# Up projection of a gated feed-forward by seven block products, with z kept in DRAM

## The reference

```python
def conv_ffn(h, w_up, conv_w, conv_b, w_down):
    s = h.shape[1]
    u = h @ w_up                                   # 1024 -> 2 x 2816
    up = jnp.pad(u, ((0, 0), (CONV_WIDTH - 1, 0), (0, 0)))
    c = conv_b
    for j in range(CONV_WIDTH):
        c = c + conv_w[j] * up[:, j:j + s]
    a, g = jnp.split(c, 2, axis=-1)
    return (jax.nn.silu(a) * g) @ w_down           # 2816 -> 1024
...
x = x + conv_ffn(rmsnorm(x, ffn_norm[l]), w_up[l], conv_w[l], conv_b[l], w_down[l])
```

## Time and profile before

| | us |
|---|---|
| median of 3 runs | 1857.29 (1854.81 to 1857.45) |
| profiled execution, its own time | 1854.01 |
| span of its instructions | 1852.2 |
| PE busy | 1758.5 (95%) |
| VectorE, ScalarE, GpSimd busy | 718.8, 576.9, 618.6 |
| mean granted TensorE clock | 0.981 of full |

### The profile page before, as it was taken

The page is one execution under the profiler, slowest core; times in us unless marked ns, Lnnn a source line. Parts: engine busy times, 40 slices in busy tenths (PEclk is TensorE's granted clock), DMA queues, the critical chain, the costliest instruction groups (busy, mean ns, idle before and its releaser), DMA issues. The chain is left out here.

```text
span 1852.2 us, 23370 instructions
## 1 busy us (share of the span) xinstructions
PE 1758.5 (95%) x8889; PEld 1437.3 (78%) x8889; DVE 718.8 (39%) x1328; ACT 576.9 (31%) x1059; POOL 618.6 (33%) x527
## 2 busy tenths in 40 slices
PE   4799999999889799999999998999999999999999
PEld 3677887877668688888888886888888888888887
DVE  5734334358874302200255222423424433442343
ACT  4435555444454323222112313221221222122121
POOL 4243564644322122222245523322331431333122
PEclk9899999999999999999999998999999999999999
DMA  5301002012200143332454502201210210220002
GB/s 192 107 18 46 25 10 63 1 35 50 67 13 1 25 115 97 106 93 80 132 165 155 184 1 80 80 14 55 68 45 23 68 54 14 68 68 27 18 24 91
DMA packets 118271, 119.29 MB, mean 64 GB/s; under 512 B 15340, under 2 KB 95916, under 8 KB 118188
## 3 DMA queue, kind: packets, MB, share of 16 engines
q1 hardware_dynamic: 118188, 118.16, 20.9%
HBM read 101.25 MB, written 16.89 MB: 64 GB/s over the span
## 5 line engine op out<-in xcount | busy, mean ns | idle before, releaser
L1900 PE MATMUL ps<-act_hi,f_hi 128*128 128x512 f32 x704 | 278.0, 395 | 6.3 <-DVE f_lo L1665 6.3
L1900 PE MATMUL ps<-act_hi,f_lo 128*128 128x512 f32 x704 | 276.9, 393 | 0.0
L1900 PE MATMUL ps<-act_lo,f_hi 128*128 128x512 f32 x704 | 274.6, 390 | 0.0
L1665 POOL TENSOR_TENSOR f_lo<-ffn_area,f_hi 128x1024 fp32r<-128x1024 f32 x65 | 155.3, 2419 | 87.5 <-ACT f_hi L1746 87.5
L1855 DVE TENSOR_TENSOR attn_out<-ps,attn_out 128x512 f32<-128x512 f32 x160 | 106.5, 686 | 136.4 <-PE ps L1920 136.4
L1900 PEld LDWEIGHTS ps<-act_hi,f_hi 128*128 128x128 f32 x704 | 132.9, 189 | 33.7 <-DVE f_lo L1665 6.7
L1900 PEld LDWEIGHTS ps<-act_hi,f_lo 128*128 128x128 f32 x704 | 132.8, 189 | 30.6
L1900 PEld LDWEIGHTS ps<-act_lo,f_hi 128*128 128x128 f32 x704 | 132.7, 189 | 29.8
L1565 PE MATMUL ps<-act_hi,g_hi 128*128 128x512 f32 x384 | 152.0, 396 | 3.1 <-DVE g_lo L1500 3.1
L1565 PE MATMUL ps<-act_hi,g_lo 128*128 128x512 f32 x384 | 151.3, 394 | 0.0
L1565 PE MATMUL ps<-act_lo,g_hi 128*128 128x512 f32 x384 | 149.7, 390 | 0.0
(11 more groups left out here) (220 smaller groups left out, 3703.2 us busy)
## 6 DMA issues: line engine op xcount, KB each, us to landing
ffn_area<-in_w_up_dram SPq DMA_DIRECT2D x44, 512.0 KB, 3.9
gates<-gate SPq DMA_DIRECT2D x24, 512.0 KB, 3.1
gate<-gates SPq DMA_DIRECT2D x24, 512.0 KB, 3.8
g_raw<-in_w_gate_dram SPq DMA_DIRECT2D x23, 512.0 KB, 4.5
ffn_area<-in_w_down_dram SPq DMA_DIRECT2D x22, 512.0 KB, 3.6
attn_out<-in_x_dram SPq DMA_DIRECT2D x16, 512.0 KB, 6.0
w_raw<-in_w_in_dram SPq DMA_DIRECT2D x16, 384.0 KB, 3.3
attn_out<-in_w_in_dram SPq DMA_DIRECT2D x16, 384.0 KB, 4.1
```

Source lines behind the costliest of these rows:

```text
L1665: eng.tensor_tensor(f_lo[:, b, :], f_raw[b], f_hi[:, b, :].bitcast(F32), ALU.subtract).then_inc(f_lo_done[b], 1)
L1900: ins = pe.matmul(ps[:, 2 * q + half, :], w[:, q, k * P:(k + 1) * P], a[:, k, half * 512:(half + 1) * 512], start=(k == 0 and i == 0), sto ...
```

## The change

`feed_forward` no longer is a block of its own. It returns functions that are called at the end of each engine's queue in `gates_and_outputs`, without a meeting of all engines, and the loops are written out.

*Up.* Of the 22 pairs (p), the first two (`PLAIN`) are computed as before: 4 groups of 24 matmuls (tile of a or g, half of the tokens), copied by ScalarE from PSUM to `u` in SBUF. The other 20 use the Winograd form of a 2 x 2 block product with 7 products in place of 8: blocks are the depth (two halves of 4 tiles), the tokens (two halves of 512) and the pair's two tiles. Each product has 4 depth tiles x 3 = 12 matmuls. Its inputs are the blocks A11, A12, A22 of the weights, four sums of them (S1 to S4, 512 columns each), the blocks of h, and four sums of those: t1, t2, t3 and t4, made once, in 20 steps of 128 x 1024 on VectorE (`combine`), cast by ScalarE and split by GpSimd (`t_high`, `t_low`, 8 of each; t4 takes the place of a block of h that the plain pairs have read). The products come in the order P1, P6, P5, P2, P7, P4, P3. ScalarE copies P1 out (`first_copy`), VectorE makes seven sums of 512 columns (U2, C11, U3, U4, C22, C21, C12) with one input in PSUM, of which four are parts of `u`. The taps then read `u` in SBUF, not PSUM; there is one conv buffer in place of two. The weight sums are made by GpSimd for p = 2 and by VectorE from p = 3 on. Parts of weights are cast and split as the place of the same part of the pair before comes free.

*z and x1.* Each z tile (512 KB) is stored to DRAM; each x1 tile too, during the output projection.

*Down.* It runs after all pairs, in two halves of the tokens (h). In each, all 8 banks hold results, and 22 slices k of 24 matmuls run over them (the last two slices together, bank by bank); nothing is added in between. z comes back from DRAM in tiles of 128 x 512 (four places, two for the split parts), w_down is loaded and split once, in the first half, into places that came free. x1 is loaded back, VectorE adds 8 results per half, SP stores 16 pieces of 256 KB.

*Start.* The first group of pair 0 stands before the last `turn`; its casts and low parts stand in the loop over the token tiles.

The diff, cut to what the text speaks of:

```diff
+                if t in (2, 3):
+                    ffn.first_high(act, t - 2)
...
+                if t in (3, 4):
+                    ffn.first_low(pool, t - 3)
+            ffn.gpsimd(pool)
...
+            ffn.tensor_first(pe)
             turn(NT - 1)
...
+    A11, A12, A22, S1, S2, S3, S4 = range(7)
+    P1, P6, P5, P2, P7, P4, P3 = range(7)
...
+    CAST_ORDER = {0: ("tile0", "tile1"), 1: ("A1", "A22", "A21"), 2: ("S2", "S34", "A1", "S1", "A22")}
+    LATER = ("S12", "A1", "A22", "S34")
...
+    LAST_READ = {P6: U2, P5: C22, P2: C11, P7: U3, P4: C21, P3: C12}
...
+    def z_place_free(eng, m):
+        if m >= 2:
+            h, k = (m - 2) // FT, (m - 2) % FT
+            if k < FT - 2:
+                eng.wait_ge(k_done, (FT - 2) * h + k + 1)
+            else:
+                eng.wait_ge(y_done, 8 * (h + 1))
...
+        for p in range(4, FT):
+            load_up(p)
+            store_z(p - 3)
...
+        store_z(FT - 1)
+        for k in range(4, FT):
+            load_wd(k)
+            load_z(k)
...
+                act.wait_ge(p_done, done(p - 1, {"S12": P5, "A1": P2, "A22": P4, "S34": P3}[part]))
...
+        def first_copy(p):
+            act.wait_ge(p_done, done(p, P1))
+            if p > PLAIN:
+                act.wait_ge(summed, summed_count(p - 1, C11))
+            act.activation(s1, bank(p, P1), ACT.Copy).then_inc(copied, 1)
+        def own_tap(p, e):
+            feature = p + e * FT
+            if p < PLAIN:
+                act.wait_ge(copied, 4 * p + 4)
+            elif e == 1:
+                act.wait_ge(summed, summed_count(p, C21))
+            else:
+                act.wait_ge(summed, summed_count(p, C12))
+            if p >= 1:
+                if e == 1:
+                    act.wait_ge(z_done, p)
                 else:
+                    act.wait_ge(z_out, 16 * p)
+            act.activation(conv[:, e, :], u[:, e, :], ACT.Identity, scale=taps[:, 2, feature:feature + 1],
+                           bias=taps[:, 3, feature:feature + 1]).then_inc(tap2_done, 1)
...
+        act.wait_ge(taps_ready, 1)
+        copy_group(0, 0)
+        for part in CAST_ORDER[1]:
+            cast(1, part)
+        copy_group(0, 1)
+        t_high(0, 0)
+        copy_group(0, 2)
+        t_high(1, 0)
+        copy_group(0, 3)
+        t_high(2, 0)
+        cast(2, "S2")
+        cast(2, "S34")
+        own_tap(0, 1)
+        own_tap(0, 0)
+        t_high(0, 1)
+        t_high(2, 1)
+        t_high(1, 1)
+        cast(2, "A1")
+        silu(0)
+        for g in range(4):
+            copy_group(1, g)
+        cast(2, "S1")
+        cast(2, "A22")
+        for r in range(2):
+            t_high(3, r)
+        for p in range(PLAIN, FT):
+            if p >= 3:
+                cast(p, "S34")
+            own_tap(p - 1, 1)
+            first_copy(p)
+            own_tap(p - 1, 0)
+            silu(p - 1)
+            if p + 1 < FT:
+                cast(p + 1, "S12")
+            if p + 1 < FT:
+                cast(p + 1, "A1")
+                cast(p + 1, "A22")
...
+        for k in range(3, FT):
+            wd_high(k)
+            z_high(k - 1)
...
+        a1, a2 = raw_tile(p, 0), raw_tile(p, 1)
+        at = 4 * (p - PLAIN)
+        eng.tensor_tensor(sums_raw[:, 0, :], a2[:, HALF[0]], a2[:, HALF[1]], ALU.add).then_inc(s_added, 1)
+        eng.tensor_tensor(sums_raw[:, 2, :], a1[:, HALF[0]], a2[:, HALF[0]], ALU.subtract).then_inc(s_added, 1)
+        eng.wait_ge(s_added, at + 1)
+        eng.tensor_tensor(sums_raw[:, 1, :], sums_raw[:, 0, :], a1[:, HALF[0]], ALU.subtract).then_inc(s_added, 1)
+        eng.wait_ge(s_added, at + 3)
+        eng.tensor_tensor(sums_raw[:, 3, :], a1[:, HALF[1]], sums_raw[:, 1, :], ALU.subtract).then_inc(s_added, 1)
...
+        for part in CAST_ORDER[1]:
+            low(pool, 1, part)
+        t_low(0, 0)
+        add_weights(pool, 2)
+        t_low(1, 0)
+        t_low(2, 0)
+        low(pool, 2, "S2")
+        low(pool, 2, "S34")
+        t_low(0, 1)
+        t_low(2, 1)
+        t_low(1, 1)
+        for part in ("A1", "S1", "A22"):
+            low(pool, 2, part)
+        t_low(3, 0)
+        t_low(3, 1)
+        for p in range(PLAIN, FT):
+            if p >= 3:
+                low(pool, p, "S34")
+            if p + 1 < FT:
+                for part in ("S12", "A1", "A22"):
+                    low(pool, p + 1, part)
+        for m in range(2 * FT):
+            z_low(m)
...
+        def other_taps(p, e):
+            dst, src, feature = conv[:, e, :], u[:, e, :], p + e * FT
+            at = 4 * p + (0 if e else 2)
+            dve.wait_ge(tap2_done, 2 * p + (1 if e else 2))
+            dve.scalar_tensor_tensor(out=dst[:, 1:S], in0=src[:, 0:S - 1], scalar=taps[:, 1, feature:feature + 1],
+                                     in1=dst[:, 1:S], op0=ALU.mult, op1=ALU.add).then_inc(tapped, 1)
...
+        dve.wait_ge(taps_ready, 1)
+        dve.wait_ge(h_lo, NT - 1)
+        dve.wait_ge(h_last, 1)
+        dve.wait_ge(x1_out, 16 * NT)
+        for r in range(2):
+            combine(r)
+        for e in (1, 0):
+            other_taps(0, e)
+        product(0)
+        for p in range(PLAIN, FT):
+            if p > PLAIN:
+                c12_sum(p - 1)
+            other_taps(p - 1, 1)
+            u2_sum(p)
+            other_taps(p - 1, 0)
+            product(p - 1)
+            if p + 1 < FT:
+                add_weights(dve, p + 1)
+            c11_sum(p)
+            u3_u4_sums(p)
+            c22_sum(p)
+            c21_sum(p)
+        for k in range(3):
+            wd_low(k)
...
+        for p in range(PLAIN, FT):
+            later = p > PLAIN
+            weights_ready(p, "A1")
+            product(p, P1, A11, act_at(0, 0))
+            weights_ready(p, "S12" if later else "S2")
+            if not later:
+                pe.wait_ge(t_lo_done, 6)
+            product(p, P6, S2, t_at(1))
+            if not later:
+                weights_ready(p, "S1")
+            product(p, P5, S1, t_at(0))
+            product(p, P2, A12, act_at(1, 0))
+            weights_ready(p, "S34")
+            product(p, P7, S3, t_at(2))
+            weights_ready(p, "A22")
+            if not later:
+                pe.wait_ge(t_lo_done, 8)
+            product(p, P4, A22, t_at(3))
+            product(p, P3, S4, act_at(1, 1))
```

More of the change, by code:

```diff
@@ L1 @@
 import math
+from collections import namedtuple
 from contextlib import ExitStack
@@ L216, in layer @@
                 wo = sb("wo", [P, 2 * NK, 2, 512], F32R, ctx=projecting)
+            with ExitStack() as ending:
+                late_slot = sb("late_slot", [P, 2, S], F32R, ctx=ending)
             ffn_area = sb("ffn_area", [P, NK, S], ctx=middle)
-            conv0, f_raw = ffn_area[:, 0:2, :], [ffn_area[:, 2 + b, :] for b in range(6)]
+            f_hi = sb("f_hi", [P, 7, 512], F32R, ctx=middle)
+            f_lo = sb("f_lo", [P, 7, 512], F32R, ctx=middle)
+            t_all = sb("t_all", [P, 3, 2, 4, 512], F32R, ctx=middle)
+            ffn = feed_forward(nc, sem, w_up, w_down, out_t, ps, act_hi, act_lo, attn_out, attn_lo, staging, taps, ffn_area,
+                               late_slot, f_hi, f_lo, t_all, f_in, out_done, x1_done, m_lo, h_lo, h_last, taps_ready)
             gates_and_outputs(nc, x_t, w_gate, b_gate, w_o_a, w_o_b, w_o_m, w_out, ffn_norm, conv_w, conv_b, w_up, ps,
@@ L221, in layer @@
                               g_raw, g_hi, g_lo, gate, bias, gates_dram, o_raw, o_hi, o_lo, merged, wo_raw, wo,
-                              x1, x1_stats, spare, ffn_area, taps, f_raw, f_in)
-            feed_forward(nc, w_up, w_down, out_t, ps, act_hi, act_lo, x1, [conv0, spare], taps, f_raw, f_in)
+                              x1, x1_stats, spare, ffn_area, taps, f_in, out_done, x1_done, m_lo, h_lo, h_last, taps_ready, ffn)
 NRAW_O = 3
@@ L1243, in gates_and_outputs @@
                       g_raw, g_hi, g_lo, gate, bias, gates_dram, o_raw, o_hi, o_lo, merged, wo_raw, wo,
[L1244 removed]
+                      x1, x1_stats, spare, staged, taps, f_in, out_done, x1_done, m_lo, h_lo, h_last, taps_ready, ffn):
     NT, NK, D = x1.shape[1], act_hi.shape[1], x1.shape[2]
@@ L1369, in _ @@
             sp.wait_ge(m_lo, NK)
-            for b in range(4):
-                load_w_up(sp, w_up, f_raw[b], b, 0, f_in)
+            for p in range(2):
+                for e in range(2):
+                    load_w_up(sp, w_up, staged, p, e, f_in)
+            for t in range(NT):
+                sp.wait_ge(x1_done, SUMS.index((t, 1)) + 1)
+                ffn.store_x1(sp, t)
+            ffn.sync(sp)
         @block.scalar
```

716 lines of the change are left out of this document (439 added, 277 removed).

## The result

The kernel after takes 1836.48 us (median of 7 runs, 1834.71 to 1845.45), the kernel before 1855.44 (7 runs, 1851.28 to 1857.45): a ratio of 0.9908, 95% interval 0.9887 to 0.9929. That is faster, by 19 us, or 0.9%: small, and clear of the noise. Forecast was 1846 with 1812 to 1874. The profiled execution of after has a span of 1834.1 and its own time is 1835.87; forecast for the two were 1841.7 and 1843.5.

What follows compares the result with a forecast made beforehand. TensorE, 95% busy, was taken as bound by the number of matmuls (3168 x 0.228 us). Steps summed to pair 3 at 1208, 18 periods to 1566, TensorE's end at 1838, span 1841.7, then 1843.5, scaled to 1846; range 1812 to 1874.

Steps and rivals of the forecast that it cites:

- Matmuls removed: Up projection: 2112 matmuls become 1872, 240 fewer at 0.228 us each, saving 54.7 us.
- The port: Feed-forward: two-SBUF-input VectorE work and GpSimd work serialise, 1.1 us and 2.35 us per 1024 columns.
- rival 1: Feed-forward: the port doesn't hold these forms, VectorE and GpSimd prepare side by side; time 1822; chance 0.15.
- The start: First groups from 1111.4; TensorE waits 19 us before pair 2 (1175); pair 3 starts at 1208.
- A later pair: Pairs from pair 3: chain through taps, silu, product, sums and low parts sets a 19.95 us period, not 19.15.
- a gap of zero: Pairs: a gap of zero per pair would show the forecast wrong; it expected 0.8 us.
- the slow clock: TensorE after waits: up to 2.2 us at the start, 3 us taken in the down part (0 to 8.8).
- The down projection: After the pairs: 1056 matmuls 241 us, three z waits 6.9, first slices 1.8, clock 3; TensorE ends at 1838.
- The recap at the end of the forecast: Whole kernel: 54.7 us saved and 10.7 gained at the start, less 31 there, 15 in pairs, 12 in down part.
- Rival 2: Pairs: bound by matmuls alone, the chain having unseen slack; 1793, median 1796; chance 0.07.
- Rival 3: Pairs: each gap of some 0.8 us brings a slow clock, period near 21.8, time 1881; chance 0.20.

Runs made afterwards that it cites:

- the two experiments on it: Against the kernel after: low part of A1 made before that of S12, 1830.92 us; one more VectorE sum per pair, 1858.32 us.
- a third place: Kernel after with a third place for the split z in the down part: 1826.87 us, ratio 0.9849 to the kernel before.
- A1 first: Kernel after with A1 ahead of S12 in ScalarE's casts and GpSimd's low parts: 1830.92 us, ratio 0.9877 to the kernel before.
- the longer chain: Kernel after with one more VectorE sum of 1.22 us per pair ahead of the weight sums: 1858.32 us, ratio 1.0023 to the kernel before.

## Why the prediction was right

The forecast of 1846 came out at 1836.5, 9.5 lower and inside its range. Of that, 7.6 us are in the profiled execution, and 1.9 in the step from there to the median (2.5 allowed, 0.6 found). The terms did not all miss the same way: most were too long, the down projection 4.0 too short, so the total is nearer than its parts.

*Matmuls removed.* 240 by the count. The price of 0.228 nearly holds in the pairs (84 in 19.28 us where nothing waits: 0.2295).

*The port.* Right, and for the form that no row of before showed: a scalar_tensor_tensor with two SBUF inputs waits (2.40 us, done 1.1 after GpSimd). That rules out rival 1, and cutting `combine` short took 17 us away, of which at least 11.6 by the port.

*The start.* The mechanism is right and the size close: 16.2 us of waiting for 19 forecast. `combine` and GpSimd together take from 1121.6 to 1172.5, 50.9 us, for 53.1 in the sum. P5 waits 2.4 (3 forecast). Pair 3 starts at 1203.5, not 1208: 2.5 us of that were there at P1 of pair 2. From that P1 to the end of ScalarE's `t_high` it took 10.8 us for 12.2 forecast, a difference that is left open; from there to P1 of pair 3 20.2 for 20.8, where the handoffs have the same fault as in the next step.

*A later pair.* This is the step that was mis-sized: 19.95 forecast, 19.43 measured. Seen from P1 at T, forecast and measured are: GpSimd done with S34 3.6 and 3.59 (1402.95); first two taps 6.1 and 5.99; the other two 9.4 and 9.10; silu 10.6 and 10.20; product passed 11.9 and 11.37; three sums 13.85 and 13.26; GpSimd begins S12 at 15.1 and 14.43; A1 split 19.95 and 19.37. All durations are right, and the last step of 4.9 too. What is wrong is five handoffs of 0.13 to 0.17 us, taken from the earlier trace rows, that measured 0.03 or 0.04. Taps follow each other in 1.31 instead of 1.43 (twice); silu follows the tap by 0.04, the product silu by 0.03, the cast the sums by 0.03. For the taps, and for a step of ScalarE behind one of VectorE, the written-out loops of before show the same fall; for the product behind silu no run does. With 0.58 us less, chain and matmuls (19.28) are all but equal, so TensorE idles 0.1 us a pair and not 0.8. The forecast had named a gap of zero as a sign of being wrong, and every second pair has one of 0.01; that the chain sets the period at all was a close thing, which only the two experiments on it show. So the 18 pairs took 6.7 us less; it would be 8.2, had the first of them not taken 1.5 us more, under the slow clock at 1203 to 1207.

*The down projection.* The three gaps, as time lost between two matmuls, were 2.49, 2.29 and 2.38 us for 2.3 forecast (the profile's idle times are 2.32, 2.12 and 2.21), and those at the first slices 0.9 and 1.0 for 1.8 in all. The slow clock came once (1691), for 1.3 us where 3 was taken. Mis-sized was the term thought safest: 1056 matmuls at 0.228 are 241 us, and they took 246 (0.2330). The earlier trace rows mix up and down matmuls: before, the up matmuls are 0.2290 apart, and the 96 of one `down`, of which these are the first and the last, 0.2273:

```profile
1256.18 0.40 PE L1920 MATMUL ps<-f_hi,z_hi 128*128 128x512 f32 x1
1277.77 0.39 PE L1920 MATMUL ps<-f_hi,z_lo 128*128 128x512 f32 x1
```

So the same 1056 matmuls became 6 us slower when z and w_down moved to other places in SBUF and into another order. The runs with a third place show that, with w_down in `t_all`, the place of z alone decides between 0.2267 and 0.2325.

*The sums.* The recap at the end of the forecast (54.7 and 10.7 less 31, 15 and 12) gives 7.4 us, while its span is 10.5 us below that of before. It leaves out the 4 us that before lost among its 3168 matmuls; the step-by-step sum is the one to go by.

*The rivals.* Rival 2 did not happen, but from pair 4 on after came within 0.15 us a pair of it, and A1 first reached it there. Rival 3 did not: idle times of 0.22, and of 1 us with the longer chain, brought no slow stretch, while 2.3 to 16.2 us did in four of the cases. The idle times of 2.12 and 2.21 us in the down part did not. A gap of that size may or may not: the one of 2.32 us was followed by a granted clock of 0.5 in after (1691), and by 1.00 in the run with the longer chain (1711.4 to 1714.8).

## What to carry to other kernels

Before work is moved between VectorE and GpSimd, count the instructions of VectorE with two SBUF inputs, and add each of them in full to GpSimd's time; a PSUM input takes an instruction out of that sum (1.28 us beside GpSimd). Where products are saved by sums, look at the first use, where all sums come at once and nothing covers them: here that wait took back 16 of 54.7 us. In a chain that returns every period, take handoffs from code of the same form (written out or looped), since five of 0.1 us decided between 19.4 and 19.95; and put what is needed first, first. When two profiles are compared, compare them part by part: unchanged code ahead of the change moved the start of the up projection by up to 4 us among after and its variants.

## What the hardware showed that was not expected

- The spacing of matmuls of one shape at a granted clock of 1.00 depends on where the operands lie: 0.2267 us with z in `f_hi` and w_down in `t_all`, 0.2325 with z in `attn_lo`, 0.2333 in after for k = 3 to 19, 0.2273 in before. Over 1056 matmuls, 0.006 us are 6 us. Which property of the places decides was not found. Nor is it the only thing: in the branch part, whose code is the same in all these kernels, the spacing was 0.2289 in after (behind its first 61 matmuls), 0.2311 in five of the other profiles and 0.2333 in three; and that of the gates was 0.2289 in all profiles but one, which had 0.2334.
- A VectorE step with two SBUF inputs waits until the GpSimd instruction in progress ends, however short it is itself: 64 columns took 2.44 us, alone 0.22.
- A tap follows the tap that it needs by 0.03 us with loops written out, by 0.15 in loops, and ScalarE follows VectorE's product by 0.03 and 0.13. The product behind a tap did not gain (0.11 and 0.10).
